# Last attention head of an encoder block: four score tiles ahead, fills from the first tile, four operand conversions moved into the head before

## The reference

```
u = rmsnorm(x); mn = rmsnorm(mem)
q = (u @ w_q_x)            -> 4 heads of 256
k, v = (mn @ w_kv_x)       -> 4 heads of 256, 256 memory tokens
scores = q k^T / 16        per head: 1024 tokens x 256 memory tokens
att = softmax(scores) v    -> 1024 x 1024
x = x + att @ w_o_x
```

## Time and profile before

| | |
|---|---|
| three runs | 2662.15, 2665.56, 2666.32 us |
| the profiled execution's own time | 2663.53 us |
| its span, first to last instruction | 2661.9 us |
| mean granted TensorE clock | 0.996 |
| TensorE busy (matmuls) | 2621.7 us |
| TensorE busy (weight loads) | 2302.5 us |
| VectorE busy | 1490.3 us |
| ScalarE busy | 866.0 us |
| GpSimd busy | 449.0 us |

### The profile page before, as it was taken

One profiled execution on the slowest core, in us unless ns is written; L12 is line 12 of the kernel. 1 busy time (PEld: TensorE's weight loads), 2 busy tenths in 40 slices (PEclk: granted clock), 3 DMA queues, 4 the chain that ended last, 5 costly groups with the idle time before them and its releaser, 6 DMA issues. The chain is left out here.

```text
span 2661.9 us, 37128 instructions
## 1 busy us (share of the span) xinstructions
PE 2621.7 (98%) x14980; PEld 2302.5 (86%) x14980; DVE 1490.3 (56%) x1762; ACT 866.0 (33%) x1022; POOL 449.0 (17%) x434
## 2 busy tenths in 40 slices
PE   7999999999999999999999999999999999999998
PEld 7888899999999999988888889977898888887887
DVE  5511100278888888554444424423348888887777
ACT  6321211234343334322223422333233434332111
POOL 3000000021122212332331001100011443430000
PEclk9999999999999999999999999999999999999999
DMA  8322232233332333434343535112212221224222
GB/s 275 121 99 95 95 119 89 93 104 103 111 102 95 102 110 102 150 119 151 126 150 130 204 125 206 32 48 79 72 64 95 101 90 65 94 80 182 104 103 79
DMA packets 166289, 297.04 MB, mean 112 GB/s; under 512 B 6971, under 2 KB 123015, under 8 KB 166176
## 3 DMA queue, kind: packets, MB, share of 16 engines
q1 hardware_dynamic: 108960, 137.13, 15.6%
q0 software_dynamic: 23248, 83.84, 9.3%
q10 hardware_dynamic: 33968, 74.52, 7.3%
HBM read 212.26 MB, written 83.20 MB: 111 GB/s over the span
## 5 line engine op out<-in xcount | busy, mean ns | idle before, releaser
L1299 DVE TENSOR_TENSOR wlo<-raw,whi 128x2048 fp32r<-128x2048 f32 x88 | 201.8, 2293 | 433.0 <-ACT whi L784 432.5
L1906 PE MATMUL ps<-whi,a_hi 128*128 128x256 f32 x1536 | 440.6, 287 | 0.5 <-DVE a_lo L1641 0.5
L1906 PE MATMUL ps<-wlo,a_hi 128*128 128x256 f32 x1536 | 435.1, 283 | 0.0
L1906 PE MATMUL ps<-whi,a_lo 128*128 128x256 f32 x1536 | 435.0, 283 | 0.0
L1875 PE MATMUL ps<-a_hi,whi 128*128 128x512 f32 x864 | 347.6, 402 | 0.2 <-DVE a_lo L1318 0.2
L1875 PE MATMUL ps<-a_hi,wlo 128*128 128x512 f32 x864 | 336.9, 390 | 0.0
L1875 PE MATMUL ps<-a_lo,whi 128*128 128x512 f32 x864 | 336.5, 390 | 0.0
L1906 PEld LDWEIGHTS ps<-whi,a_hi 128*128 128x128 f32 x1536 | 295.1, 192 | 1.4 <-DVE a_lo L1641 0.7
L1906 PEld LDWEIGHTS ps<-wlo,a_hi 128*128 128x128 f32 x1536 | 295.4, 192 | 0.4 <-issue 0.2
L1906 PEld LDWEIGHTS ps<-whi,a_lo 128*128 128x128 f32 x1536 | 295.1, 192 | 0.0
L789 ACT ACTIVATE ev<-ps 128x512 f32<-128x512 f32 x208 | 124.4, 598 | 508.5 <-PE ps L1875 290.3
(11 more groups left out here) (337 smaller groups left out, 5110.5 us busy)
## 6 DMA issues: line engine op xcount, KB each, us to landing
raw<-in_w_in SPq DMA_DIRECT2D x45, 1024.0 KB, 5.2
raw<-in_w_up SPq DMA_DIRECT2D x22, 1024.0 KB, 5.1
hg_T<-ev ACTq DMA_DIRECT2D x24, 512.0 KB, 2.7
qfb<-hg_T POOLq DMA_DIRECT2D x24, 512.0 KB, 5.0
hidden_T<-ga ACTq DMA_DIRECT2D x11, 1024.0 KB, 4.0
raw<-in_w_down SPq DMA_DIRECT2D x11, 1024.0 KB, 7.0
s<-hidden_T SPq DMA_DIRECT2D x11, 1024.0 KB, 4.9
raw<-in_w_kv_x SPq DMA_DIRECT2D x8, 1024.0 KB, 6.4
```

The lines of the kernel that those rows point to most:

```text
L1299: signal(dve, dve.tensor_tensor(wlo[:, b.slot], w4[:, b.slot], whi[:, b.slot], ALU.subtract), w_lo, b.count())
L1906: ins = pe.matmul(ps[:, u, part * BC:(part + 1) * BC], op[sw][:, k, t * P:(t + 1) * P], W[mw][:, b.slot, k], start=k == 0 and q == 0, stop ...
```

## The change

It touches the last head (and the end of the third). Four tiles of scores lead instead of six, in banks 4, 5, 2 and 3; tile t's transposes are followed by the scores of tile t + 4, and tiles 4 to 7 use banks 4 and 5 in turn. The groups of output products stand at t = 0 and 1 (units 0 and 1, pieces 0 and 1, then 2 and 3), at t = 4 and 5 (the same for units 2 and 3), at t = 7 (units 0 and 1, piece 4) and after tile 7 (units 2 and 3, piece 4); before, they stood at t = 4 to 7 and after. Pieces 0 to 3 are converted at the end of the third head: on ScalarE 0 and 1 before the copies of its attended values, 2 and 3 between the two copies; on VectorE all four behind tile 7's normalising. Pieces 4 and 5 stay in the last head, at t = 4 and 5 on ScalarE and t = 5 and 6 on VectorE.

```
 def score_bank(r):
-    return 4 + r % 2 if r < NT * (X_HEADS - 1) or r % NT > 5 else r % NT
+    return (4, 5, 2, 3)[r % NT] if r >= NT * (X_HEADS - 1) and r % NT < 4 else 4 + r % 2
...
 # ScalarE
-                    if j == X_HEADS - 1 and 2 <= t < NT:
-                        operand_hi(3 * KT + t - 2, a_hi, a_raw)
+                    if j == X_HEADS - 1 and t in (4, 5):
+                        operand_hi(3 * KT + t, a_hi, a_raw)
...
                 for u in range(4) if j < X_HEADS - 1 else ():
                     act.wait_ge(a_sc, 8 * j + 8)
                     unit_out(Blk(B_Q + j + 1), u)
+                for k in range(2) if j == X_HEADS - 2 else ():
+                    operand_hi(3 * KT + k, a_hi, a_raw)
...
                     if j < X_HEADS - 1:
                         signal(act, act.activation(atS[:, d], attended, ACT.Copy), a_ev, 2 * j + 1 + d)
+                        for k in range(2, 4) if d == 0 and j == X_HEADS - 2 else ():
+                            operand_hi(3 * KT + k, a_hi, a_raw)
...
 # VectorE
-                    if j == X_HEADS - 1 and t >= 3:
-                        operand_lo(3 * KT + t - 3, a_hi, a_lo, a_raw)
+                    if j == X_HEADS - 1 and t in (5, 6):
+                        operand_lo(3 * KT + t - 1, a_hi, a_lo, a_raw)
                     if j < X_HEADS - 1 and t == NT // 2 + 1:
                         split_lo(Blk(B_Q + j + 2))
+                for k in range(4) if j == X_HEADS - 2 else ():
+                    operand_lo(3 * KT + k, a_hi, a_lo, a_raw)
...
 # TensorE
+            O_FILL = {0: ((0, 1), range(0, 2)), 1: ((0, 1), range(2, 4)), 4: ((2, 3), range(0, 2)), 5: ((2, 3), range(2, 4)),
+                      7: ((0, 1), range(4, 5)), NT: ((2, 3), range(4, 5))}
...
-                    elif t >= NT:
-                        for u in range(4):
-                            half_N(Blk(B_O), u, 0, opA, 3 * KT, range(4, 5))
-                    elif t >= NT // 2:
-                        ks = range(0, 2) if t < NT // 2 + 2 else range(2, 4)
-                        for u in (0, 1) if t % 2 == 0 else (2, 3):
+                    elif t in O_FILL:
+                        us, ks = O_FILL[t]
+                        for u in us:
                             half_N(Blk(B_O), u, 0, opA, 3 * KT, ks)
...
-                    if j and t == (4 if last else 0):
+                    if j and t == 0:
                         pe.wait_ge(a_ev, 2 * j - 1)
-                    if r >= 2 and not (last and t < 6):
+                    if last and t in (4, 5):
+                        pe.wait_ge(a_exp, r - 3)
+                    elif r >= 2 and not (last and t < 4):
                         pe.wait_ge(a_exp, r - 1)
...
-                lead = 6 if last else 2
+                lead = 4 if last else 2
...
-                    if t + 2 in range(lead, NT):
-                        scores(t + 2)
+                    if t + lead < NT:
+                        scores(t + lead)
```

## The result

The changed kernel takes 2669.83 us, the median of 20 runs (2665.76 to 2673.87), against 2665.62 us for the kernel before in its 20 runs (2662.02 to 2669.2). That is 4.2 us more. The ratio is 1.0016, with a 95% interval of 1.001 to 1.0022: slower beyond what scatter explains, by about 0.16%. The forecast was 2.6 us more, 2668.2, in a range of 2663.0 to 2672.0.

A forecast was written before the change was run, and what follows sets the result against it. TensorE, busy for 98% of the span, was taken to bound the kernel. A chain 0.9 us later plus 1.7 us for one clock fall gave 2.6 us over the 2665.56 median: 2668.2 us, range 2663.0 to 2672.0.

The forecast's parts named there:

- The conversions: End of head three: ScalarE waits for the load until 1855.1, so the store of head three issues 3.4 us late.
- The banks of the scores: Last head's start: first scores wait for the d=0 copy to free banks 4 and 5, a new 1.5 us gap.
- Scores 6 and 7: Last head, TensorE: these scores wait for the exponentials of tiles 4 and 5, gaps of 1.3 and 2.4 us.
- The second half: Last head's later tiles: tile 6's transposes wait until 1879.85, a 2.6 us gap; values start at 1882.0.
- The chain's total: Last head: the product with the values starts 0.9 us later than before, with ends of 0.4 and 1.1.
- The clock: TensorE in the last head: one fall to half clock for 3.4 us behind the new gaps, costing 1.7 us.
- The rival with both falls: Last head: clock falls after scores 7's and tile 6's gaps, costing 5.1, with 0.9 totalling 6.0 us (2671.6); chance 0.11.
- The edits at nothing: After the last head's scores: w_o loads start 3.4 us later and GpSimd's next order moves with them, at no cost.
- The bound of 7.9 us: The 24.0 us stretch: less 5.0 of gaps and 2.9 of clock, 16.1 is true work; 7.9 is the most gainable.
- Gaps closed: Last head: fills close the gaps and the clock holds, gaining up to 7.9 us (2657.7); chance 0.06.
- Clock holds: Last head: no fall to half clock, so only 0.9 us is lost, giving 2666.5; chance 0.17.
- A late first load: End of head three: first load lands with the second, 2.6 us later, 5.2 us lost in all (2670.8); chance 0.04.

The follow-up runs named there:

- run 1: Kernel before with only the change's conversions of pieces 0 to 5, TensorE's order and banks unchanged: 0.8 us over before (2666.78 us, ratio 1.0004).
- run 3: Changed kernel with ScalarE copying the attended values of d=0 before the four conversions: 4.2 us over before (2670.12 us, ratio 1.0014).
- run 5: Changed kernel with scores of tiles 6 and 7 one tile later, behind transposes of tiles 3 and 4: 2.4 us under before (2663.83 us, ratio 0.9993).
- run 4: Changed kernel with 9 spare matmuls in each gap, before scores 7 and before tile 6's transposes: 1.1 us over before (2667.1 us, ratio 1.0009).
- run 8: Changed kernel with the fill of tile 5 moved before the transposes of tile 6: 2.3 us over before (2668.53 us, ratio 1.0013).
- 12: Changed kernel with tile 5's fill moved before tile 6's transposes and spare matmuls in both long gaps: 1.75 us over before (2667.89 us, ratio 1.0006).
- run 6: Kernel before with 6 and 12 spare matmuls in its gaps before the transposes of tiles 2 and 3: 1.65 us under before (2664.6 us, ratio 0.9995).
- the second profile: Changed kernel itself, unaltered, run and profiled again beside the experiments: 5.0 us over before (2671.14 us, ratio 1.0012), stretch 27.55 us.
- 2: Kernel before with only the change's scores order and banks, fills and conversions unchanged: 1.5 us over before (2667.49 us, ratio 1.0005).
- run 7: Changed kernel with a new order of scores, banks, copies, conversions and fills, d=0 copied first: 2660.36 us, 5.9 under before (ratio 0.9981).

## Why the prediction was right, and where its sizes were off

*The conversions.* Right to a tenth. Less the 3.01 us by which the stretch stands later, ScalarE's first conversion started at 1855.14 (said: 1855.1), the copy of d = 0 ended at 1858.34 (1858.35), that of d = 1 at 1861.57 (1861.6), and VectorE's first maximum started at 1862.05 (1862.1). That ScalarE's free time was no cover, since the load lands behind it, is shown by its 4.21 us of waiting. What it is worth is less than the prediction's place for it suggests: alone it costs 0.8 us (run 1, not told from nothing), and undone in the change 0.35 us of the stretch (run 3).

*The banks of the scores.* First scores at 1858.48 (1858.4), the wait 1.41 (1.5), named for the copy as forecast.

*First fills.* Transposes of tile 0 at 1864.19 (1864.0), the wait 0.59 (0.6).

*Scores 6 and 7.* At 1869.35 (1869.3) and 1872.92 (1872.8), the waits 1.13 and 2.22 (1.3 and 2.4). Of the steps moved alone this one weighs most: it took the stretch from 28.62 to 22.22 and the time from 4.2 us over before to 2.4 under, though its interval still takes in no difference (run 5).

*The second half.* The transposes of tile 6 came at 1882.18, not 1879.85, with the clock's loss in between; with the clock held (run 4) their gap is as forecast, 2.5 us, of which the spare matmuls take 2.05. The prediction calls it a gap in which nothing fills; runs 8 and 12 show that a fill doesn't help, since it is the end of a chain over ScalarE and VectorE.

*The chain's total.* 0.9 was said, 1.06 is measured (run 4), inside its ends of 0.4 and 1.1. The steps themselves gave 1882.0, 1.07 later than before, which is what run 4 shows. The prediction took off a part because its pitches gave 1881.4 for the order of before where the row says 1880.93; it doesn't say at which clock, and with the clock held that order ends at 1856.92 + 22.13 = 1879.05 (run 6). So the pitches fit the new order and missed the old one by up to 2.35 us, and how well the 0.9 came out owes something to luck. Also, the comparison mixes two things: before's 24.01 had 1.9 us of half clock in it (run 6), so against like the order costs 2.9.

*The clock.* This term was mis-sized. I took one fall of 3.4 us, 1.7 us. The profile has two, 3.55 us, the second profile 27.55 - 25.07 = 2.5, and the medians 4.2 - 1.1 = 3.1. The rival with both falls (5.1, given 0.11) had the right picture, though the longer fall came first and not second, and the forecast had one fall too few. Its two falls cost less than 5.1 us: of the 10.2 us at half clock TensorE worked through 8.8 (from 1875.93 to 1881.56 and from 1885.19 to 1888.38), half of which is 4.4, and where it next waited for another engine, before the transposes of tile 6, some of the loss was taken up. So the time came out between the two, inside the range. The prediction went by the length of the time at half clock behind one gap in another stage and not by the number of new gaps. Its row without a fall, the 3.23 us gap, was one execution's chance: that gap stands in all 14 profiles of this record, and the clock fell in it or behind it in 11. It also says that the clock of before fell after the two gaps; it fell inside the second, which ended at 1867.67 where the fall is at 1866.72. With both gaps open the clock fell twice in three of four profiles (the change's two and run 3; once in run 8), and with both filled it stayed (runs 4 and 12). The Trainium skill (TensorE: Matmul & The Clock Gate, A second HAM failure mode) says that short idles between groups of matmuls let the clock swing between its two levels. These traces agree, at 2.5 to 3.55 us for the change's two gaps.

*The edits at nothing.* Behind the stretch the waits of TensorE are those of before, so the late w_o loads cost nothing: 781.0 us follow the stretch in each of the three profiles in which the clock doesn't fall behind it (before, 2 and 4).

*The bound of 7.9 us.* It was a little too high: 16.1 us of true work were said, and run 7 shows 17.3 busy at full clock, which leaves 6.7. Most of the error is the 2.9 us taken off for the clock where 1.9 were lost.

*The rivals.* Gaps closed: refuted for this order, and true for another (run 7). Clock holds: measured as run 4, 1.1 us over before where 0.9 was said. A late first load: landings of 4.8 and 6.9 us again in the change's profile, no case of it.

## What to carry to other kernels

When an engine's work is moved ahead, look in its in-order list for what stands behind the first place at which it can now wait: here `scores(7)` waited for an exponential that needed transposes queued in front of it to be copied first, and one tile's delay of that order was worth 5.3 to 6.4 us of a 28 us stretch, 2.85 of them with the clock held. A gap on TensorE can have two prices here, its own length and up to half of what TensorE then works at 1.2 GHz; fill it with spare matmuls once, as a measurement, and the difference is the second price. And where runs scatter by more than the effect, compare a stretch between two marks that both kernels have, not spans.

## What the runs showed of the hardware

The same gap brings half clock in one execution and none in the next. For five of the gaps, how often and for how long over the 14 profiles:

| gap on TensorE | profiles that have it | of these, with a fall in or behind it | us at 1.2 GHz |
|---|---|---|---|
| until about 1112, 2.08 us | 14 | 12 | 3.4 |
| until about 1470, 1.2 to 1.9 us | 14 | 6 | 3.4 |
| before scores 7, unfilled, 2.2 to 2.3 us | 5 | 5 | 3.4 or 6.8 |
| before tile 6, unfilled, 2.1 to 2.5 us | 5 | 3 | 3.4 |
| until about 2417, 3.2 us | 14 | 11 | 3.4 or 6.8 |

The last row also prices a fall in another stage. From the last head's product to the end it is 781.0 us in three profiles without a fall, 782.4 to 782.7 in six with one of 3.4 us, and 783.7 to 783.9 in five with one of 6.8 us, so 1.4 to 1.7 and 2.7 to 2.9 us. A price for such a gap can only be given as a range. Also unexpected was that 18 spare matmuls in gaps made two stretches shorter, that of the change by 2.5 to 3.55 us and that of the kernel before by 1.9.
